# State-space rounds of a two-block transformer: decay sums from one 32-row matmul, and the time step multiplied into x for each direction

## The reference, cut to what matters

```python
dt = jax.nn.softplus(dt_raw ... + dt_bias)          # 2 directions x 32 heads
dt_f, dt_b = dt[:, :, 0], dt[:, :, 1]
y_fwd = ssd_chunked(xf * dt_f[..., None], dt_f * A[0], bm, cm)
y_bwd = flip(ssd_chunked(flip(xf * dt_b[..., None]), flip(dt_b * A[1]), flip(bm), flip(cm)))
y = y_fwd + y_bwd + ssd_D[:, None] * xf

# in ssd_chunked(X, A, B, C), for each chunk, group and head
CB = einsum(C, B)                                   # tokens x tokens, one per group
M = CB * exp(segsum(A))                             # exp(cs[l] - cs[s]) below the diagonal
y_diag = M @ X
states = einsum(B, exp(cs[-1] - cs), X)
y_off = einsum(C, carried state, exp(cs))
```

## Time and profile before

| | |
|---|---|
| executions shown, us | 928.28, 920.29, 919.83; median 920.29 |
| profiled execution, span, us | 926.9 |
| mean granted TensorE clock | 0.996 |
| TensorE busy | 903.5 us, 97% |
| VectorE busy | 668.4 us, 72% |
| ScalarE busy | 512.5 us, 55% |
| GpSimd busy | 79.8 us, 9% |

### The profile page before, as it was taken

How to read it: one execution, slowest core, us unless ns; L and a number is a source line. 1 busy time by engine, 2 the same in 40 slices (tenths; PEclk the granted TensorE clock), 3 DMA queues, 4 the chain that set the end, 5 groups by cost and what they waited for, 6 DMA issues and landing times.

```text
span 926.9 us, 18052 instructions
## 1 busy us (share of the span) xinstructions
PE 903.5 (97%) x7424; PEld 859.7 (93%) x7424; DVE 668.4 (72%) x918; ACT 512.5 (55%) x696; POOL 79.8 (9%) x56
## 2 busy tenths in 40 slices
PE   5999999999999999999999999999998999999998
PEld 3899998788888899999999999988898999999998
DVE  6877998997699988778766545555875856666642
ACT  2566666667878773445655443346576754444430
POOL 0133000010465330000000000000000000000000
PEclk9999999999999999999999999999999999999999
DMA  9764554766322237684755555544332435555650
GB/s 376 302 242 151 204 192 147 263 219 236 124 65 87 92 138 250 223 301 146 264 182 182 186 188 193 192 152 169 116 126 86 142 137 187 185 190 193 217 192 18
DMA packets 25084, 168.00 MB, mean 181 GB/s; under 512 B 2868, under 2 KB 4532, under 8 KB 5048
## 3 DMA queue, kind: packets, MB, share of 16 engines
q1 hardware_dynamic: 23760, 164.90, 50.4%
q10 hardware_dynamic: 1256, 2.12, 0.6%
HBM read 165.95 MB, written 1.06 MB: 180 GB/s over the span
## 4 chain that ended last, share of the span: by engine, by line
PE 78%; DVE 8%; ACT 7%; issue 3%; DMA 3%; POOL 0%; SPq 0%; DVEq 0%; ACTq 0%; POOLq 0%
PE bank L1864 77%; DVE wlo L1107 2%; ACT whi L573 2%; DMA raw<-w_stream 2%; DVE acc L1152 1%; DMA adas<-w_stream 1%; ACT kw__113 L822 1%; PE bank L2132 1%; DVE eb L1432 1%; ACT ew L789 0%; DVE sslo L1468 0%; DVE wlo L1117 0%; DVE cvt L1341 0%; DVE p L1319 0%; ACT prob L724 0%
## 5 line engine op out<-in xcount | busy, mean ns | idle before, releaser
L1864 PE MATMUL bank<-hhi,whi 128*128 128x256 f32 (+1 forms) x1364 | 384.5, 284 | 0.8 <-DVE hlo L1210 0.6
L1864 PE MATMUL bank<-hlo,whi 128*128 128x256 f32 (+1 forms) x1352 | 377.5, 280 | 0.0
L1864 PE MATMUL bank<-hhi,wlo 128*128 128x256 f32 (+1 forms) x1352 | 375.7, 280 | 0.0
L1107 DVE TENSOR_TENSOR wlo<-raw,whi 128x2048 fp32r<-128x2048 f32 (+1 forms) x130 | 299.0, 2301 | 101.1 <-ACT whi L573 99.2
L573 ACT ACTIVATE whi<-raw 128x2048 fp32r<-128x2048 f32 (+1 forms) x132 | 250.6, 1898 | 101.3 <-PE bank L1864 74.2
L1864 PEld LDWEIGHTS bank<-hhi,whi 128*128 128x128 f32 (+1 forms) x1364 | 256.3, 188 | 11.5 <-issue 10.4
L1864 PEld LDWEIGHTS bank<-hlo,whi 128*128 128x128 f32 (+1 forms) x1352 | 257.2, 190 | 0.1
L1864 PEld LDWEIGHTS bank<-hhi,wlo 128*128 128x128 f32 (+1 forms) x1352 | 253.6, 188 | 0.0
L1864 PE MATMUL bank<-fhi,whi 128*128 128x256 f32 x432 | 121.4, 281 | 0.0
L1864 PE MATMUL bank<-flo,whi 128*128 128x256 f32 x432 | 121.4, 281 | 0.0
L1864 PE MATMUL bank<-fhi,wlo 128*128 128x256 f32 x432 | 121.4, 281 | 0.0
(11 more groups left out here) (296 smaller groups left out, 1311.2 us busy)
## 6 DMA issues: line engine op xcount, KB each, us to landing
raw<-w_stream SPq DMA_DIRECT2D x147, 1024.0 KB, 4.9
adas<-w_stream SPq DMA_DIRECT2D x8, 1024.0 KB, 8.6
xres<-x_t SPq DMA_DIRECT2D x1, 1024.0 KB, 10.1
out<-oute SPq DMA_DIRECT2D x8, 128.0 KB, 3.4
tabs<-tabs_in_dram ACTq DMA_DIRECT2D x1, 641.0 KB, 8.5
tabs<-tabs_in_dram ACTq DMA_DIRECT2D x1, 512.0 KB, 3.7
hankel<-bucket_rows ACTq DMA_DIRECT2D x1, 512.0 KB, 10.9
cols<-cols_in_dram ACTq DMA_DIRECT2D x1, 325.0 KB, 8.0
```

The source lines that it names most:

```text
L1107: nc.vector.tensor_tensor(out=wlo[:, c % RING, 0:n], in0=raw[:, r % RING, 0:n], in1=whi[:, c % RING, 0:n].bitcast(f32), op=ALU.subtract)\
L1864: return nc.tensor.matmul(out, lhsT, rhs, start=start, stop=stop)
```

## The change

Its parts:

1. The prefix sums are laid out in 16 copies of 8 heads, 32 rows a group: 16 rows of cs and 16 rows that become -1 and +1 or the like. GpSimd makes from them two operands (`row_roles`: `css` and `csr`, two instructions of 128x512), so that one matmul of the group's 32 rows holds both terms of a difference. `decays` has two matmuls in place of four. Its columns are still 512.
2. `pair_rows` (GpSimd, 128x512, twice in all) adds rows of two heads, so that the row sums for the carried state take one matmul of 32 rows. `group_halves` is gone (8 small GpSimd instructions).
3. dt is no longer multiplied into the masked products but into x: `scaled(i)` on GpSimd, two instructions of 128x512 a round (`xback` = x times backward dt, then x times forward dt in place). The 8 ScalarE and 8 VectorE instructions a round are gone; VectorE now multiplies the decays by each masked CB (two instructions of 128x1024 a round). `outputs_own` has 16 head matmuls in place of 8. The identity matmul stays.
4. The two masks are one VectorE instruction. `eb` is gone: maximum and exponential are taken in place in `ew`, which ScalarE may write again only when the products of the round before are made.
5. VectorE does `decayed_products` ahead of the attention gate product.
6. New tiles lie in the space of `xres`, so ScalarE's queue loads x (1 MB) again after the last round, and VectorE waits for it before wo.

```diff
             def own_rows(t, d):
                 nc.gpsimd.tensor_tensor(out=bd[:, d * HG:(d + 1) * HG, :],
-                                        in0=spread(csr[:, t, :].bitcast(f32), 1, HG),
+                                        in0=spread(csr[:, 2 * t + d, :].bitcast(f32), 1, HG),
...
+            def row_roles():
+                nc.gpsimd.tensor_scalar(css[:, :, :], csr[:, :, :].bitcast(f32), marks[:, 0, 1:2], marks[:, 1, 0:1],
+                                        ALU.mult, ALU.add).then_inc(csr_done, 1)
+                pool.wait_ge(csr_done, 3)
+                nc.gpsimd.tensor_scalar(csr[:, :, :], csr[:, :, :].bitcast(f32), marks[:, 0, 0:1], marks[:, 0, 1:2],
+                                        ALU.mult, ALU.add).then_inc(csr_done, 1)
+            def pair_rows(t):
...
+                nc.gpsimd.tensor_tensor(out=pairs_[:, :, :], in0=own[:, 0], in1=own[:, 1], op=ALU.add)\
+            def scaled(i):
+                g, t = i % NG, i // NG
+                if i >= 1:
+                    pool.wait_ge(yd_done, i)
+                x = xtok[:, t, g * 512:(g + 1) * 512].rearrange("p (h d) -> p h d", d=HD)
+                nc.gpsimd.tensor_tensor(out=xback[:, :].rearrange("p (h d) -> p h d", d=HD), in0=x,
...
+                nc.gpsimd.tensor_tensor(out=x, in0=x, in1=spread(dtk[:, t, g * HG:(g + 1) * HG], 2, HD),
+                                        op=ALU.mult).then_inc(xs_done, 1)
...
             for i in range(8):
-                group_halves(i)
...
                 decayed(i)
+                if i == 0:
+                    scaled(0)
                 if i < NG:
                     skipped(i)
                 if i >= 2:
+                    scaled(i - 1)
                     weighted(i - 2)
                     if i == NG - 1:
                         pool.wait_ge(segf_done, NG)
                         own_rows(1, 0)
+                        pair_rows(1)
                     squares(i - 2)
...
+            scaled(7)
...
             def iteration_exps(i):
                 act.wait_ge(segf_done, i + 1)
                 if i >= 1:
-                    act.wait_ge(late_done, 2 * i)
+                    act.wait_ge(w_done, 2 * i)
...
-            def iteration_weights(i):
...
-                for h in range(HG):
-                    nc.scalar.activation(kw_[:, h, :], cbf[:, :], ACT.Copy,
-                                         scale=dtk[:, t, g * HG + h:g * HG + h + 1]).then_inc(kf_done, 1)
...
                     act.dma_start(tabs2[:, :], tabs2_dram).then_inc(tabs2_in, 16)
+                    act.dma_start(xres[:, :, :], x_dram).then_inc(x_in, 16)
...
                 if i == 11:
-                    dve.wait_ge(csr_done, 4)
-                    for d in range(2):
-                        rows = slice(2 * NH + d * NH, 2 * NH + (d + 1) * NH)
-                        nc.vector.tensor_tensor(out=csr[rows, :, :], in0=side[3][rows, :].rearrange(
...
+                    nc.vector.scalar_tensor_tensor(out=rows, in0=rows.bitcast(f32), scalar=marks[:, 2, 1:2],
+                                                   in1=side[3][:, :], op0=ALU.mult, op1=ALU.add).then_inc(csr_done, 1)
                     dve.wait_ge(dexp_done, 1)
-                    step(nc.vector.tensor_tensor(out=dec[:, 0, :], in0=dec[:, 0, :], in1=dtk[:, 0, 0:NH],
-                                                 op=ALU.mult))
...
             def decayed_products(i):
...
-                for h in range(HG):
-                    dve.wait_ge(kf_done, HG * i + h + 1)
-                    step(nc.vector.scalar_tensor_tensor(
...
-                nc.vector.tensor_tensor(out=kw2, in0=kw2, in1=eb[:, :], op=ALU.mult).then_inc(w_done, 1)
+                for d, into in ((0, kw_), (1, kwb)):
+                    nc.vector.tensor_tensor(out=into[:, :, :], in0=ew[:, :, :], in1=spread(cb2[:, d, :], 1, HG),
+                                            op=ALU.mult).then_inc(w_done, 1)
...
             dve.wait_ge(mod_done, 3)
+            dve.wait_ge(x_in, 32)
...
                     for t in range(NT):
-                        for part in range(2):
-                            last = mm(side[3][part * 2 * NH:(part + 1) * 2 * NH, t * 2 * P:(t + 1) * 2 * P],
-                                      dta[:, t, :], masks)
+                        for d, mask in ((0, "le"), (1, "ge")):
+                            last = mm(side[3][:, (2 * t + d) * P:(2 * t + d + 1) * P], dtax[:, 2 * t + d, :],
+                                      tab(mask))
...
-                for part in range(2):
-                    own = bd[:, (1 - t) * HG:(2 - t) * HG, :].rearrange("p (j two) l -> p two j l", two=2)[:, part]
-                    last = mm(side[4][:, :], grp[:, i % 2, HD - part * HD:HD - part * HD + P], own, part == 0, part == 1)
-                last.then_inc(bc_done, 1)
+                rows = slice(g * 4 * HG, (g + 1) * 4 * HG)
+                mm(side[4][:, :], par[rows, :], pairs_[rows, :, :]).then_inc(bc_done, 1)
...
+                rows = slice(g * 4 * HG, (g + 1) * 4 * HG)
                 for k in range(2):
-                    heads = d * NH + g * HG + 4 * k
-                    mm(side[k][:, :], group(g, P), bd[:, d * HG + 4 * k:d * HG + 4 * k + 4, :], True, False)
-                    last = mm(side[k][:, :], csr[:, t, :], spread(ind[:, heads:heads + 4], 2, P), False, True)
+                    last = mm(side[k][:, :], css[rows, 2 * t + d, :], bd[rows, d * HG + 4 * k:d * HG + 4 * k + 4, :])
                 last.then_inc((segf_done, segb_done)[d], 1)
...
                 mm(side[5][:, :], tab("ident"), xcv[:, 4 * g:4 * g + 4, t * P:(t + 1) * P], True, False)
-                for h in range(HG):
...
+                pe.wait_ge(xs_done, 2 * (i + 1))
+                for d, (x, first, w) in enumerate(((xtok[:, t, :], g * HG * HD, kw_), (xback, 0, kwb))):
+                    pe.wait_ge(w_done, 2 * i + d + 1)
+                    for h in range(HG):
...
```

157 lines of the change are left out of this document (76 added, 81 removed).

## The result

| | before | after |
|---|---|---|
| median of 20 executions each, us | 922.64 (914.97 to 932.66) | 933.63 (925.20 to 942.85) |
| ratio, 95% interval | | 1.0104, 1.0078 to 1.0130 |
| profiled execution, span, us | 926.9 | 926.8 (its own time 928.64) |
| mean granted TensorE clock | 0.996 | 0.989 |

The forecast was 922.7 with a range of 916 to 928 and 0.88 on "within 1%". The two medians differ by 11.0 us; the ratios of this document leave out executions more than 1.5% above the fastest of their kernel (here one of the kernel after and three of the kernel before), and this one means +9.6 us (0.0104 x 922.64). That is four times the +2.4 of the sum, and the median lies outside the range. 2.3 us of the distance to the forecast are not the change's: the kernel before has a median of 922.64 here, and the prediction knew three executions with one of 920.29.

The account below looks back on a forecast made before the run. TensorE was taken to bound the rounds, with VectorE just behind. Terms -9.0 + 7.0 + 5.8 - 0.35 - 0.7 - 0.3 gave +2.4 us on a median of 920.29, so 922.7 us, range 916 to 928.

Parts of the forecast that it names:

- the sum: Whole program: all terms on TensorE's path added up to +2.4 us.
- TensorE bounds the rounds, and distances between starts are the price: Rounds: TensorE sets the pace at 11.8 us a round, VectorE just behind, so changes are priced in distances on TensorE.
- -9.0 and +7.0: Rounds on TensorE: 40 decay and row-sum matmuls removed save 9.0 us; 64 head matmuls added cost 7.0 us.
- The something else, +5.8: Rounds on TensorE: 16 blocks of 32-row matmuls cost 0.36 us each beyond their columns, for changing tile shape.
- Rival 1: Rounds on TensorE: no price for 32-row blocks, so 5.8 falls out, giving -3.4 and 916.9 us; chance 0.15.
- The two small terms: Prefix-sum matmuls lose one shape block, -0.35 us; TensorE's wait at the end of xbc shrinks, -0.3 us.
- The fifth round, -0.7: Fifth round: the copy to `ew` comes 2 us earlier on a freer ScalarE, removing TensorE's 0.7 us wait.
- Rival 2: Rounds: GpSimd and VectorE obstruct each other, VectorE becomes the bound; up to 947 us, half partial at 924 to 929; chance 0.13.
- The reload, 0 us with "7.5 us of cover for 2.7": In so: reloading x takes 2.7 us of the DMA rings, hidden by 7.5 us before TensorE needs the delayed chunk.

Follow-up runs that it names:

- e1_full_rows: The changed kernel with decay and row-sum matmuls taking all 128 rows in place of the group's 32 (output not the reference's); 928.45 us, ratio 1.0080.
- e8_blocks_joined: The changed kernel with x reloaded at the last chunk of the rounds and the backward decays moved behind the head matmuls; 930.09 us, ratio 1.0062.
- e13_gate_no_scaling: The changed kernel with early x reload, the attention gate's sigmoid moved ahead of the row-sum exponential, and no `scaled`; 929.71 us, ratio 1.0120.
- e10_before_gate_early: The kernel before with only the attention gate's sigmoid moved ahead of the row-sum exponential; 923.04 us, ratio 0.9992.
- e3_early_reload: The changed kernel with the reload of x issued at the last chunk of the rounds; 928.68 us, ratio 1.0067.
- e2: The kernel before with x loaded again behind the tables in the first so chunk, VectorE waiting for it before wo; 927.58 us, ratio 1.0005.
- e9: The changed kernel with early x reload and the attention gate's sigmoid moved ahead of the row-sum exponential; 931.37 us, ratio 1.0053.
- e12: The changed kernel with early x reload, backward decays behind the head matmuls, and the gate's sigmoid ahead of the row-sum exponential; 927.51 us, ratio 1.0009.
- e14: The changed kernel with early x reload, backward decays behind the heads, gate's sigmoid ahead of the row-sum exponential, and `pair_rows(1)` on VectorE; 925.24 us, ratio 1.0012.

## Why the prediction was wrong, point by point

- **TensorE bounds the rounds, and distances between starts are the price: right.** Steady rounds in all traces add up from them.
- **-9.0 and +7.0: right.** e1_full_rows: 11.54 us against the 11.50 that follow from them at the same distance of the split matmuls; the heads take 1.90 us where 1.9 was named.
- **The something else, +5.8: right in kind, a little small.** 0.41 a block against 0.36, just above the bound of 0.39: +6.6 us. It was read from 64-row tiles. The first of two such matmuls also takes longer to the next (0.34 us, 312.60 to 312.94, where 0.21 to 0.23 was named). Rival 1 is refuted. e8_blocks_joined adds what is paid for: one change of shape less gave 0.20 us. The rule of the Trainium skill (page "TensorEngine Tiling (Array Packing)", section "Key Properties") that a change of tiling mode drains the engine agrees with this.
- **The two small terms: right in kind.** The wait at the end of xbc fell by 0.6 us (1.31 to 0.72), twice the 0.3 named. The prefix sums gave 0.23 and not 0.35: from the product ahead of them to the next small product of the mixer and attention (both ahead of the table above) the two traces take 4.40 and 4.17 us.
- **The steady part** was +3.1 us (the sum without its -0.7). Measured: 83.98 - 80.93 = +3.05 for the rounds without any hole (e13_gate_no_scaling against e10_before_gate_early), +1.65 behind the last state product, -0.54 ahead of the first and -0.23 for the prefix sums, +3.9 in all. With the measured prices of blocks, xbc and prefix sums the forecast's sum would be +3.8.
- **The fifth round, -0.7: this step failed.** The text said that ScalarE is freer, so the copy to `ew` comes 2 us earlier, and that `pair_rows(1)` adds 1.04 us "with GpSimd idle for half of a round". Measured: before 1.0 us lost at the turn (81.96 - 80.93), after 4.2 (88.21 - 83.98), so +3.2 instead of -0.7; 1.5 of it is the half clock that the same hole did not bring in e3_early_reload. Two errors made it. GpSimd's instructions were priced alone (1.04), though the 2.80 of the earlier trace rows showed what standing beside each other does to both engines; `pair_rows` took 3.13, `yw` 2.02. And ScalarE's list was not read on from the squares: behind the wait stood 4.48 us of sigmoid and table loads, and behind them all that TensorE needed. What the runs show in its place: the hole goes only when the sigmoid leaves this chain and the scalings leave GpSimd (e13_gate_no_scaling, 24.85 us for the two rounds).
- **Rival 2 (chance 0.13) had the mechanism, at the wrong place.** The products took 12 us more over the rounds than counted (16.5 + 15.2 - 16 x 1.23), 1.5 us a round, and VectorE stood at 9.3 of 10 and not below 9. Under the 2 us named as deciding, and so it cost a steady round nothing. But an average over eight rounds says nothing of the one in which GpSimd also has its rows to make.
- **The reload, 0 us with "7.5 us of cover for 2.7": doubtful.** It landed 6.1 us after its issue, and the cover counted was that of one chunk. In the trace the loss shows in wo and norm, 30 us and more after the landing, where ScalarE waits for weight chunks in every kernel. Some 3 us, not settled: e10_before_gate_early lost as much without it.
- **The sum.** +3.9, +3.2 and about +3 make some 10, against +9.6 measured; only the first is shown to hold in every execution, since the other two hang on falls of the clock and on the weight stream. The three misses (+0.8, +3.9 and about +3) have one sign, which the range, built around single terms, didn't allow for.

## What to carry to other kernels

Price an instruction on GpSimd by what it takes beside a busy VectorE: in the changed kernel's trace 1.3 to 1.8 times its time alone on the mean, three times at worst. And look for the round that has extra work, not at the mean round. Where a stall is expected to go, follow the late engine's list to the end: what stands behind the wait in the same queue (here a sigmoid between two table loads) comes as late as the wait ends, and moving it into the idle time ahead takes most of it out of the chain. Matmuls saved by a new tile shape can cost back most of what they saved: 3 x 0.225 us went out of the forward gap and 0.27 came of it, 2 x 0.225 behind the state product and 0.04. And before two traces are compared for a few tenths of a us, compare the distance of their like matmuls and their falls of the clock.

## What the runs showed of the hardware that was not expected

- The distance between 256-column matmuls is 113 or 118 ns at full granted clock. Behind the rounds it mostly stays at one of them for a whole phase: gu 121.7 or 126.1 us, dn 59.7 or 62.1, m2 to the scores of the second block 130.3 or 133.8. In the rounds it changes from one half chunk to the next. Which it is changes from execution to execution: dn took 62.07 us in the traces of the kernel before, e2, e9, e12 and e14, and 59.73 in e10, the kernel before with one instruction moved. It makes 10 us over a program, as much as the change does, and is likely the main reason why 12 executions gave intervals 0.6 to 1.0% wide.
- A hole of 1 to 3.5 us is sometimes followed by some us at half the granted clock, and sometimes not: the fifth round's hole of 2.4 us was in the changed kernel and wasn't in e3_early_reload, at the same place; that of 3.38 us in e1_full_rows was, and that of 3.43 us in e8_blocks_joined wasn't. At the norm behind wo all but two of the sixteen traces have such a fall, of 3 us (the kernel before) to 10 us (the changed kernel and six others).
- The sums of squares (128x512) on GpSimd took 1.27 to 3.32 us, VectorE's product of 128x1024 from 1.21 to 2.92, and its weight split of 128x2048 from 2.28 to 3.46; the long ones are those beside the other engine.
